# Later quarter sums as transposes and row reductions, and a narrower mixing product, in a fused two-block kernel on Trainium2

## What is computed

```python
mod = jax.nn.silu(c) @ w_ada[l] + b_ada[l]
shift1, scale1, gate1, shift2, scale2, gate2 = jnp.split(mod, N_MOD, axis=-1)
h = rms_norm(x, norm1_w[l]) * (1.0 + scale1[:, None]) + shift1[:, None]
proj = h @ w_in[l]
u_pool, q, k, v, g_a, g_b = jnp.split(proj, split_at, axis=-1)
y_a = multiscale_pool(u_pool, w_pool[l], pool_scale[l]) @ w_a_up[l]
```

## Time and profile before

| | us |
|---|---|
| median of 3 runs | 2575.79 |
| lowest and highest of them | 2573.85, 2578.29 |
| the profiled execution, its own time | 2573.49 |
| its span in the trace | 2571.7 |
| PE busy | 2508.2 (98%) |
| DVE busy | 2018.9 (79%) |
| ACT busy | 1276.9 (50%) |
| POOL busy | 266.9 (10%) |
| moved by DMA | 663.66 MB, 258 GB/s on average |

### The profile page before, as it was taken

One profiled execution on the slowest core, in us unless ns is written; L12 is line 12 of the kernel. 1 busy time (PEld: TensorE's weight loads), 2 busy tenths in 40 slices (PEclk: granted clock), 3 DMA queues, 4 the chain that ended last, 5 costly groups with the idle time before them and its releaser, 6 DMA issues.

```text
span 2571.7 us, 32612 instructions
## 1 busy us (share of the span) xinstructions
PE 2508.2 (98%) x12429; PEld 2107.0 (82%) x12429; DVE 2018.9 (79%) x2305; ACT 1276.9 (50%) x1657; POOL 266.9 (10%) x313
## 2 busy tenths in 40 slices
PE   6999999999999999999999999999999999999999
PEld 5878787877888888888887878888888888888887
DVE  6778889998988898889877788886766666665566
ACT  4544455444555445544545554566455544554453
POOL 1000120202020202020300001450000000020000
PEclk9999999999999999999999999999999999999999
DMA  9999869997989898989757766465566777766664
GB/s 346 333 343 330 295 196 351 330 333 247 323 296 347 289 363 278 359 292 356 267 182 228 229 197 184 152 212 171 186 212 233 224 232 232 230 212 196 191 192 157
DMA packets 298876, 663.66 MB, mean 258 GB/s; under 512 B 20752, under 2 KB 21104, under 8 KB 297696
## 3 DMA queue, kind: packets, MB, share of 16 engines
q1 hardware_dynamic: 296128, 652.31, 74.9%
q0 software_dynamic: 2016, 7.56, 0.8%
q10 hardware_dynamic: 576, 1.70, 0.2%
HBM read 659.39 MB, written 2.10 MB: 257 GB/s over the span
## 4 chain that ended last, share of the span: by engine, by line
PE 83%; DVE 8%; issue 3%; ACT 3%; DMA 3%; POOL 0%; SPq 0%; DVEq 0%; ACTq 0%
PE PS L651 82%; DVE WL L1526 2%; ACT WH L1113 2%; DVE ACC L1534 2%; DVE UQ L1526 1%; DMA RAWX<-in_w_in 1%; PE PS L654 1%; DMA RAW<-in_w_in 0%; DMA RAWX<-in_w_o 0%; DMA RAW<-in_w_ada 0%; DVE AL L1526 0%; DVE hn L1534 0%; DMA RAW<-in_w_ff 0%; ACT AH L1113 0%; DVE HL L1534 0%
## 5 line engine op out<-in xcount | busy, mean ns | idle before, releaser
L1113 ACT ACTIVATE WH<-RAW 128x1024 fp32r<-128x1024 f32 x569 | 602.5, 1059 | 767.3 <-PE PS L651 590.0
L1526 DVE TENSOR_TENSOR WL<-RAW,WH 128x1024 fp32r<-128x1024 f32 x569 | 707.7, 1245 | 341.1 <-ACT WH L1113 339.9
L651 PE MATMUL PS<-WH,AH 128*128 128x512 f32 x2052 | 811.0, 395 | 17.5 <-DVE WL L1526 10.0
L651 PE MATMUL PS<-WH,AL 128*128 128x512 f32 x2052 | 799.9, 390 | 0.0
L651 PE MATMUL PS<-WL,AH 128*128 128x512 f32 x2052 | 799.7, 390 | 0.0
L651 PE MATMUL PS<-HL,WH 128*128 128x512 f32 x2048 | 644.1, 396 | 6.2 <-DVE HL L1534 5.1
L651 PEld LDWEIGHTS PS<-WH,AH 128*128 128x128 f32 x2052 | 385.7, 188 | 103.8 <-DVE WL L1526 18.1
L651 PEld LDWEIGHTS PS<-HL,WL 128*128 128x128 f32 x2048 | 384.7, 188 | 90.8
L651 PEld LDWEIGHTS PS<-WH,AL 128*128 128x128 f32 x2052 | 385.5, 188 | 81.8
L651 PEld LDWEIGHTS PS<-WL,AH 128*128 128x128 f32 x2052 | 386.1, 188 | 76.4 <-issue 0.2
L651 PE MATMUL PS<-HL,WL 128*128 128x256 f32 x2048 | 402.4, 278 | 0.0
(11 more groups left out here) (250 smaller groups left out, 1962.0 us busy)
## 6 DMA issues: line engine op xcount, KB each, us to landing
RAW<-in_w_ff SPq DMA_DIRECT2D x337, 512.0 KB, 4.4
RAW<-in_w_ada SPq DMA_DIRECT2D x282, 512.0 KB, 5.1
RAW<-in_w_in SPq DMA_DIRECT2D x192, 512.0 KB, 4.6
RAWX<-in_w_ada SPq DMA_DIRECT2D x102, 512.0 KB, 5.4
RAWY<-in_w_ff SPq DMA_DIRECT2D x96, 512.0 KB, 4.2
RAWX<-in_w_ff SPq DMA_DIRECT2D x79, 512.0 KB, 5.4
RAWX<-in_w_in SPq DMA_DIRECT2D x48, 512.0 KB, 5.4
RAW<-in_w_out SPq DMA_DIRECT2D x32, 512.0 KB, 3.6
```

Of the source, the lines that this page charges most:

```text
L651: return e.matmul(o, l, r, start=start, stop=stop, skip_group_check=True)
L1113: return e.activation(o, i, f, **kw)
L1526: return e.tensor_tensor(o, a, b, op)
```

## The change

For quarters 1, 2 and 3 PE no longer multiplies the `ACC` blocks by ones. It transposes the eight 128x128 blocks (`turn`, a product with the identity in transpose mode) into two full banks of PSUM, 512 columns each. DVE then adds along the rows: two reductions of 4 x 128 columns into four columns each, and each reduction is followed by a wait for its own result (`s_qr`) and by the bias addition. Quarter 0 stays as it was. In `pool_mix` the product of the first 128 tokens takes 144 columns in place of 256; the mixing matrix is zero in the other 112.

```diff
                 if q > 0:
                     e.wait_ge(s_mod, 3 * summed(q, 0) - 3)
+                if q > 0:
+                    for g in range(2):
+                        for k in range(4):
+                            at = 1024 * (q % 2) + 512 * g + 128 * k
+                            m = turn(PS[:, 6 + g, 128 * k:128 * k + 128], ACC[:, at:at + 128])
+                    m.then_inc(s_sum, 1)
+                    return
                 for k0, k1 in sum_parts(q):
...
-                    mm(o, UQ[:, 0, 0, col:col + 128], m0, c == 0, False)
+                    mm(o[:, 0:144], UQ[:, 0, 0, col:col + 128], m0[:, 0:144], c == 0, False)
                     m = mm(o[:, 128:256], UQ[:, 0, 1, col:col + 128], m1, False, True)
...
                         bias = BC[:, 16 * g + 4 * q + k0:16 * g + 4 * q + k1]
+                        if q > 0:
+                            red(MOD[:, row, cols_q], heads(PS[:, 6 + g, :]), ALU.add).then_inc(s_qr, 1)
+                            e.wait_ge(s_qr, 2 * q + g - 1)
+                            tt(MOD[:, row, cols_q], MOD[:, row, cols_q], bias, ALU.add).then_inc(s_mod, 1)
+                            continue
                         tt(MOD[:, row, cols_q], PS[:, 6 + (k0 > 0), 4 * g + k0:4 * g + k1], bias, ALU.add).then_inc(s_mod, 1)
```

More of the change, by code:

```diff
@@ L574, in program @@
         s_half = sem("first_half_done")
+        s_qr = sem("quarter_reduced")
         s_fc, s_fr, s_fs, s_fl, s_fp = sem("f_low_part"), sem("f_relu"), sem("f_square"), sem("f_lo"), sem("f_gated")
```

## The result

The changed kernel takes 2571.55 us in the median of 22 runs (2567.12 to 2573.18), the kernel before 2575.09 us in the median of 22 runs beside them (2571.42 to 2578.29). The ratio is 0.9984 with a 95% interval of 0.9978 to 0.9990, or -4.1 us (-5.7 to -2.6). A second comparison in another job gave 0.9991 (0.9983 to 1.0000), -2.3 us. So the kernel is faster by 2 to 4 us, where the forecast said 1.5: inside its range of times, with both ratios within 0.2%, and on the right side, but short of the gain by a third to two thirds. Of the 2.75 us between the 2574.3 us of the forecast and the 2571.55 us measured, 0.7 us are the kernel before's own: its median is 2575.09 us here and was 2575.79 us in the three runs that the forecast went by.

What follows compares the result with a forecast made beforehand. TensorE was taken as the bound from 42 us on, though not throughout, as it waits at places. Landing -0.6, quarter 3 -0.91 and mix 0 gave -1.5 us: 2575.8 - 1.5 = 2574.3 us, range 2570.5 to 2578.3 us.

Steps and rivals of the forecast that it cites:

- TensorE's 0.91 us per quarter: Quarters 1 to 3: eight transposes take 0.79 us in place of 1.70 us, saving TensorE 0.91 us each.
- VectorE's 1.45 us: Quarters 1 to 3: two reductions and their waits add 1.45 us on VectorE, 0.80 of it covered by earlier release.
- Rival B: At quarters 2 and 3 VectorE's longer hold decides; a loss above 2.36 us added, +1.1 us at 2.9; chance 0.14.
- Chunk 44: Quarter 2, TensorE waiting for AL: starts 0.75 us earlier, not 1.82, and idles some 1.4 us in place of 0.38.
- The landing near 180 us: Weight chunk landing at 180.37 us that ends TensorE's wait at 182.74: moves by -0.6 us, ends -0.26 and -1.4.
- Quarter 3: TensorE saves another 0.91 us, to -1.5 us; VectorE's 0.65 us are covered by 1.87 us of idle time.
- The mix at nothing: Pooled branch: the narrower mixing product saves TensorE 0.37 us a group, 1.5 us over four, but gains nothing in time.
- Rivals C and D: C: transposes take two passes, 2576.9 us, chance 0.05; D: transposes act like idle time for the clock, 2579.4 us, chance 0.02.
- The sum: Whole kernel: -0.6 - 0.91 + 0 = -1.5 us, so 2574.3 us.

Runs made afterwards that it cites:

- hold_twice: The changed kernel with every row reduction of quarters 1 to 3 made twice, the first result thrown away; ratio to the kernel before 0.9994 (0.9985 to 1.0003).
- before_pool_early: The kernel before with GpSimd's two pooled-branch loads let go one pair of AL earlier; ratio to the kernel before 0.9995 (0.9986 to 1.0004).
- mix_only: The kernel before with only the mixing product narrowed to 144 columns, sums still products with ones; ratio to the kernel before 1.0007 (0.9998 to 1.0016).
- turns_only: The changed kernel with the mixing product back at 256 columns, so transposes and row reductions alone; ratio to the kernel before 0.9994 (0.9986 to 1.0002).
- after_feed_first: The changed kernel with VectorE making its ACC and WL pieces before waiting for a quarter's sum; ratio to the kernel before 0.9992 (0.9983 to 1.0001).
- before_feed_first: The kernel before with VectorE making its ACC and WL pieces before waiting for a quarter's sum; ratio to the kernel before 0.9996 (0.9987 to 1.0004).
- before_pool_late: The kernel before with GpSimd's two pooled-branch loads held until all AL are made; ratio to the kernel before 1.0008 (0.9999 to 1.0017).
- before_again: The kernel before run once more with no edit; ratio to the kernel before 0.9998 (0.9990 to 1.0007).

## Why the prediction was right, and where it was not

**TensorE's 0.91 us per quarter**: right, three times over. The eight transposes take 0.79 us, and the lead grows by 0.92 to 0.95 at quarters 1, 2 and 3 in both traces of the changed kernel (the first: from -2.03 to -2.95 between 185 and 217 us, which is quarter 3's).

**VectorE's 1.45 us**: right to the hundredth. The reduction out of PSUM takes 0.688 us where 0.68 was read off two rows of other shapes, and the hold is 1.80 - 0.35 us. The next `ACC` went from 155.82 to 155.51, -0.31 for a forecast of -0.26. Rival B needed more than 2.36 us added. hold_twice had 2.64 and still wasn't slower than before: B overstated quarter 3 (0.37 us against the 0.9 that 2.64 - 1.76 gives) and didn't know that a loss at chunk 44 comes back.

**Chunk 44**: right in kind. TensorE starts 1.07 us earlier and idles 1.23 us, for 0.75 and 1.4. VectorE lost its idle time ahead of that `WL` altogether (161.38 in place of 162.44), and so gained 0.3 us more than I had counted.

**The landing near 180 us**: right in direction, mis-sized, and outside its own range. "The transfers get their first buffer 0.26 us earlier, later ones up to 1.8 us earlier ... I take -0.6 us, with -0.26 and -1.4 as ends" was measured as -2.05 us in the first trace and as -1.7 us on average over three kernels with transposes and three without. By the prediction's own test, a landing that moves by under 1.4 us, this was a miss. I had leaned to the first freed buffer, and had read the gap that can be closed off one stretch (0.88 at 171 to 174 us, 0.3 us). But the gap at 156 to 158 us, which went from 157 down to 29 GB/s, costs nothing: filling it moved nothing forward. And the shortfall that was closed is longer than that stretch: 297 against 367 GB/s over 165 to 173 us, worth 1.5 us. There the later buffers count, the transfer of chunk 50 being issued 1.68 us earlier, which is the "up to 1.8 us" of the prediction. And 1.8 MB that GpSimd asks for lie right ahead of the landing; I had looked at SyncE's queue and not at GpSimd's. They are why it is late at all (4.3 to 4.9 us), and their start moves it (before_pool_early). But it moves by 1.99 us under the change without them too, so their earlier start is not shown to be the cause of the 2 us.

**Quarter 3**: right. -0.91 us more, with VectorE's hold covered by its idle time.

**The mix at nothing**: right. Its savings turn up as idle time ahead of `PT`, one row of before going from 0.21 to 0.58 us, the 0.37 us forecast, and mix_only shows no gain.

**Rivals C and D**: neither came. The transposes are one record each. The granted clock was 1.00 behind all of them. It fell only behind waits of TensorE, between 1.78 and 3.08 us long, which the last section takes up.

**The sum**: with -1.7 for -0.6 it would have been -2.6 us. The lead at 284 us says -2.1, or -2.7 without turns_only's fall of the clock. With this term at a third of what was measured the forecast held because its range is wide (2570.5 to 2578.3 us): the error of 1.1 us is small beside the scatter of the runs, and the time alone says nothing for or against the step. The second comparison says -2.3 us, the first -4.1 with its upper end at -2.6. What lies between 2.3 and 4.1 isn't settled: behind 400 us the two traces of before differ from each other by up to 2.6 us, and that of turns_only loses 3.7 and 5.2 us against the two of the changed kernel, so no cause of that size can be read from single traces. Nor do the medians settle it: turns_only's interval (0.9986 to 1.0002) and the changed kernel's overlap. Part of it may be the clock: a kernel that waits less at 180 us has fewer occasions for the fall. That was seen in single executions and is not shown for the medians.

## What to carry to other kernels

When a transfer ends a wait, list everything that lies ahead of it in all queues, with what gave each its go, before one buffer is made its cause; here 1.8 MB of what lay ahead came from an engine that nobody watched. And when a cause has been found by taking it away, do the same in the changed kernel: the landing moved by 2 us under the change with the loads and without them, and only the pair of runs tells that. A gap in the transfers costs only if the next thing waited for would have used it. And a bulk load that nobody needs for 70 us should start where TensorE has no wait for a landing: started at 226 us it cost 6.4 us of lead by 250 us, half of them by the clock; at 204 us it cost between nothing and 1.1 us in three traces. Its worth in the time of the whole kernel is not resolved here, since the intervals with and without overlap.

## What the runs showed of the hardware that I had not expected

**The clock falls behind a wait of some 2 us, but not always.** Waits of TensorE between 42 and 300 us and the granted clock behind them: 2.08 (hold_twice, at 164.49), 2.00 (turns_only), 2.44 (after_feed_first), 3.08 (before_feed_first) and 2.30 us (before_pool_late, at 241.91) were each followed by a stretch at the lower level. Those of 1.81 (before), 2.33 and 2.13 (mix_only, the second at 295.42) and 2.08 us were not, this last one in before_again:

```profile
182.50 0.50 PE L651 MATMUL PS<-WH,AH 128*128 128x512 f32 x1 [2.08 <-DVE WL L1526]
```

The same 2.08 us of idle time cost 1.7 us more in one execution and nothing in the other. Further on it fell behind shorter waits too (1.78 us at 1287.89 in turns_only). So a wait of this size has a price that a single trace of it can't give. Near 535 us TensorE waits 2.06 to 2.11 us. Behind that wait the level fell in before_again and in both traces of the changed kernel, but not in the first of before, which puts about 1.7 us between single traces of the same program. The Trainium skill ("TensorE: Matmul & The Clock Gate", Part 4: PE-mode transpose) says that transposes don't count as busy for the clock in the way products do. No run here had a fall behind eight of them in a row, nor behind the 16 that the prediction names.

**One landing scatters by itself.** From the issue of GpSimd's loads to the landing behind them it took 12.3 to 14.1 us in ten traces, in two of the same kernel 12.79 and 13.08, or 12.66 and 13.33. TensorE waits for this landing in nine of the ten, so a forecast of its place there can't be better than some 0.7 us to either side.
